# Both gates' input projections moved to the start of a hybrid decoder layer, cut into quarters of the contraction, and the gated merge put on GpSimd

## What is computed

```python
mod = silu(c) @ w_ada + b_ada                  # six vectors of 2048: shift, scale, gain for two sub-layers
h = rmsnorm(x, g_pre_mix) * (1 + sc_m) + sh_m
hq, hf, hi, hg, cq, ckv, kr, gate_a, gate_b = split(h @ w_in)
y_a = hgrn2(hq, hf, hi, hg) @ w_o_hg           # gated linear recurrence, 16 heads
y_b = attention(cq, ckv, kr) @ w_o_mla         # latent attention, 16 heads
merged = sigmoid(gate_a) * y_a + sigmoid(gate_b) * y_b
x = x + ga_m * rmsnorm(merged @ w_out, g_post_mix)
h = rmsnorm(x, g_pre_ffn) * (1 + sc_f) + sh_f
x = x + ga_f * rmsnorm((silu(h @ w_gate) * (h @ w_up)) @ w_down, g_post_ffn)
```

## Time and profile before

| | us |
|---|---|
| median of three runs | 2020.46 |
| span of the profiled execution | 2021.7 |
| TensorE busy in it | 1871.2 (93%) |
| VectorE busy | 1342.2 (66%) |
| ScalarE busy | 877.7 (43%) |
| GpSimd busy | 115.0 (6%) |
| moved by DMA | 421.8 MB, 209 GB/s in the mean |

### The profile page before, as it was taken

One profiled execution on the slowest core, in us unless ns is written; L12 is line 12 of the kernel. 1 busy time (PEld: TensorE's weight loads), 2 busy tenths in 40 slices (PEclk: granted clock), 3 DMA queues, 4 the chain that ended last, 5 costly groups with the idle time before them and its releaser, 6 DMA issues.

```text
span 2021.7 us, 26141 instructions
## 1 busy us (share of the span) xinstructions
PE 1871.2 (93%) x8954; PEld 1562.8 (77%) x8954; DVE 1342.2 (66%) x1484; ACT 877.7 (43%) x974; POOL 115.0 (6%) x77
## 2 busy tenths in 40 slices
PE   1539999999999999999999996999999999999996
PEld 1428888788878887888787785788888888888885
DVE  7876777687777776777777645655555555555554
ACT  4125364446445643554434443444444443444342
POOL 0000031004000400040000000000000000000000
PEclk8769999999999999999999998999999999999998
DMA  8885754784477448645777654455565555555552
GB/s 320 305 293 192 277 177 148 243 292 161 156 273 269 146 161 287 230 156 167 270 266 276 216 192 172 151 193 188 188 194 189 192 189 191 192 190 187 196 188 73
DMA packets 116225, 421.77 MB, mean 209 GB/s; under 512 B 12976, under 2 KB 13104, under 8 KB 115888
## 3 DMA queue, kind: packets, MB, share of 16 engines
q1 hardware_dynamic: 116144, 420.70, 61.5%
HBM read 418.55 MB, written 2.10 MB: 208 GB/s over the span
## 4 chain that ended last, share of the span: by engine, by line
PE 78%; DVE 9%; DMA 8%; issue 3%; ACT 1%; DVEq 0%; SPq 0%; POOL 0%; ACTq 0%; POOLq 0%
PE PS L677 23%; PE PS L679 23%; PE PS L678 23%; DMA ada_raw<-in_ada 5%; DVE ada_acc L1077 3%; PE PS L862 2%; DMA raw<-in_ada 2%; DVE ada_acc L987 2%; PE PS L686 1%; DVE wlo L973 1%; PE PS L807 1%; PE PS L806 1%; DMA raw<-in_w_c 1%; PE PS L712 1%; ACT whi L377 0%
## 5 line engine op out<-in xcount | busy, mean ns | idle before, releaser
L973 DVE TENSOR_TENSOR wlo<-raw,whi 128x1024 fp32r<-128x1024 f32 (+1 forms) x600 | 734.2, 1228 | 436.6 <-ACT whi L377 427.8
L377 ACT ACTIVATE whi<-raw 128x1024 fp32r<-128x1024 f32 (+1 forms) x600 | 629.7, 1053 | 821.9 <-PE PS L679 675.3
L677 PE MATMUL PS<-whi,hT_hi 128*128 128x512 f32 x1664 | 662.6, 398 | 55.4 <-DVE hT_lo L1057 40.6
L679 PE MATMUL PS<-whi,hT_lo 128*128 128x512 f32 x1664 | 653.0, 392 | 0.0
L678 PE MATMUL PS<-wlo,hT_hi 128*128 128x512 f32 x1664 | 652.8, 392 | 0.0
L677 PEld LDWEIGHTS PS<-whi,hT_hi 128*128 128x128 f32 x1664 | 316.0, 190 | 123.5 <-DVE hT_lo L1057 40.9
L679 PEld LDWEIGHTS PS<-whi,hT_lo 128*128 128x128 f32 x1664 | 315.4, 190 | 67.1
L678 PEld LDWEIGHTS PS<-wlo,hT_hi 128*128 128x128 f32 x1664 | 316.3, 190 | 63.4
L987 DVE SCALAR_TENSOR_TENSOR ada_acc<-ada_raw,csilu,ada_acc 128x512 f32<-128x512 f32 x240 | 180.1, 750 | 55.1 <-DMA ada_raw<-in_ada 50.1
L677 PE MATMUL PS<-whi,oT_hi 128*128 128x512 f32 x480 | 187.6, 391 | 2.4 <-DVE oT_lo L1433 2.4
L679 PE MATMUL PS<-whi,oT_lo 128*128 128x512 f32 x480 | 187.2, 390 | 0.0
(11 more groups left out here) (194 smaller groups left out, 1438.4 us busy)
## 6 DMA issues: line engine op xcount, KB each, us to landing
ada_raw<-in_ada SPq DMA_DIRECT2D x128, 512.0 KB, 4.7
raw<-in_w_gate SPq DMA_DIRECT2D x88, 512.0 KB, 3.3
raw<-in_w_up SPq DMA_DIRECT2D x88, 512.0 KB, 3.3
raw<-in_w_down SPq DMA_DIRECT2D x88, 512.0 KB, 3.3
raw<-in_ada SPq DMA_DIRECT2D x64, 512.0 KB, 4.8
raw<-in_w_hf SPq DMA_DIRECT2D x32, 512.0 KB, 5.5
raw<-in_w_hq SPq DMA_DIRECT2D x32, 512.0 KB, 4.8
raw<-in_w_hi SPq DMA_DIRECT2D x32, 512.0 KB, 4.4
```

The source lines that it names most:

```text
L377: nc.scalar.activation(whi[:, pl.slot(c), 0:w], raw[:, pl.slot(c), 0:w], ACT.Copy)\
L677: nc.tensor.matmul(o, hi[:, kt, tok], whi[:, s, cols], start=start, stop=False)
L679: last = nc.tensor.matmul(o, lo[:, kt, tok], whi[:, s, cols], start=False, stop=stop)
L973: nc.vector.tensor_tensor(wlo[:, s, 0:w], raw[:, s, 0:w], whi[:, s, 0:w].bitcast(F32), ALU.subtract)\
```

## The change

The gates' projections leave the stage of their own and join the latent projections at the start. `w_start` holds, for each quarter of the channels (four k-tiles, two chunks), ten column groups: 2 for cq and ckv, 4 for gate b, 4 for gate a. So the start multiplies 80 chunks in place of 16, in four phases of 20; each phase adds partial sums of two chunks to buffers in SBUF (ScalarE copies in the first phase, VectorE adds in the other three), and sigmoid is taken in place in the last. The gates lie where `ya` and `yb` lay (`gate`), and a new buffer `merged` takes the sum: in the loop VectorE multiplies each output projection by its gate into `scaled`, and GpSimd adds that to `merged`.

A chunk of `w_ada` is now one k-tile of 128 rows by 1024 columns (still 512 KB, one instruction of VectorE in place of two). At the start it goes through four slots of its own, 16 chunks before the first phase and 16 beside the first 16 weight chunks of each of the phases 0 to 2. In the loop 32 chunks go beside c = 3 to 18 and c = 24 to 39 (`ADA_AT`) in place of 24 beside c = 3 to 26. Transposes and gain spreading move between the chunks of the output projection. The masks become bytes, and `pTx` shares memory with `qT`.

```diff
-ADA_A = 3
+ADA_A = 2
+ADA_W = 2 * NW
+ADA_SLOTS = 4
+PH = 4
+SG = 2 + 2 * GD
+W_G = CD // PH
...
+        ADA_AT = [3, 3 * CD]
...
+            def load_ada0(a):
+                if a >= ADA_SLOTS:
+                    sp.wait_ge(ada_step, a - ADA_SLOTS + 1)
+                sp.dma_start(ada0_slot[a % ADA_SLOTS], ada0[a]).then_inc(ada_loaded[a % ADA_SLOTS], 16)
...
             def load(pl, c, src, width=NW):
 
-                sp.wait_ge(lo_ready, pl.through(c) - RING)
+                if not pl.starts(c):
+                    sp.wait_ge(lo_ready, pl.through(c) - RING)
...
+            start = place_c()
+            for c in range(RING):
+                load(start, c, w_start[c])
+            for n in range(PH):
+                for i in range(SG * W_G):
+                    a = (n + 1) * KD + i
+                    if i < KD and a < ADA0:
+                        load_ada0(a)
+                    c = n * SG * W_G + i + RING
+                    if c < N_C:
+                        load(start, c, w_start[c])
...
+                    for d in range(ADA_A):
+                        a = c - ADA_AT[d] - LEAD
+                        if 0 <= a < KD:
+                            load_ada(g, d * KD + a)
...
+                def merge(n):
+
+                    p = pl.pair(8 + n)
+                    pool.wait_ge(pair_free[p], pl.freed(8 + n) + 1)
+                    cols = merged[:, :, n % GD * NW:(n % GD + 1) * NW]
+                    pool.wait_ge(sig("merges"), g * (2 * GD) + (n + 1))
+                    nc.gpsimd.tensor_tensor(cols, cols, scaled[n % 2], ALU.add).then_inc(sig("merges"), 1)
...
+            sum_quarter(0)
+            for n in range(PH):
                 pe.wait_ge(sig("h_low"), (n + 1) * KP_Q)
-                for j in range(2):
-                    multiply(pl, j, CD, 2 * n + 2 * j, 2 * n, 2 * n + 2, hT_hi, hT_lo)
+                for j in range(SG):
+                    multiply(pl, n * SG + j, W_G, (n * SG + j) * W_G, 0, W_G, hT_hi, hT_lo, kt0=n * W_G * KC)
+                    if j == 7 and n < PH - 1:
+                        sum_quarter(n + 1)
...
+            for c in range(CD):
+                pe.wait_ge(sig("m_low"), c + 1)
+                multiply(pl, 0, CD, 0, c, c + 1, hT_hi, hT_lo)
+                if c + 4 < CD:
+                    transpose_merged(c + 4)
+            for j in range(1, GD):
+                if j <= 2:
+                    spread_gain(j)
+                multiply(pl, j, CD, j * CD, 0, CD, hT_hi, hT_lo)
...
+            for a in range(KD):
+                ada0_chunk(a)
+                if a == 3 * KD // 4:
+
+                    dve.wait_ge(sig("x_squared"), TT)
+                    nc.vector.tensor_scalar(stat[:, 0:TT], stat[:, 0:TT], 1.0 / D, EPS, ALU.mult, ALU.add)\
+                      .then_inc(sig("trunk_mean"), 1)
+            shift_and_scale(0)
+            tables()
+            quarter_low(0)
...
+            for c in range(N_C + AHEAD):
+                low(pl, c)
+                n, i = divmod(c, SG * W_G)
+                if i < KD and (n + 1) * KD + i < ADA0:
+                    ada0_chunk((n + 1) * KD + i)
+                if i == SG * W_G - 1 and n < PH - 1:
+                    shift_and_scale(n + 1)
+                    quarter_low(n + 1)
+                j, odd = divmod(c - AHEAD, W_G)
+                if odd == W_G - 1 and SG <= j:
+                    add_pair(pl, j, c - AHEAD, start_sum[j % SG])
...
-                        i = c - A_ADA
-                        if 0 <= i < ADA_A * CD:
-                            j = i // CD
-                            if i == 2 * CD:
-
-                                dve.wait_ge(sig("ada_summed_a"), g + 1)
-                            ada_chunk(g * ADA_A + j, i % CD, j % 2)
+                        for d in range(ADA_A):
+                            a = c - ADA_AT[d]
+                            if 0 <= a < KD:
+                                if d and a == 0:
+
+                                    dve.wait_ge(sig("ada_summed_b"), g + 1)
+                                ada_chunk(g, d * KD + a)
...
-                        add_pair(pl, 8 + n, c - 3, sums_of[:, :, (n % GD) * NW:(n % GD + 1) * NW])
+                        dve.wait_ge(sig("gate_ready"), 2 * GD)
+                        dve.wait_ge(multiplied, pl.through(c - 3))
+                        if n == 1:
+                            dve.wait_ge(sig("cross_scored"), g + 1)
+                        if n >= 2:
+                            dve.wait_ge(sig("merges"), g * (2 * GD) + n)
+                        p = pl.pair(8 + n)
+                        nc.vector.tensor_tensor(scaled[n % 2], banks(2 * p), start_sum[2 + n], ALU.mult)\
+                          .then_inc(pair_free[p], 1)
```

More of the change, by code:

```diff
@@ L416, in _, with scale_quarter @@
             pl = place_c()
-            for n in range(QUARTERS):
-                for c in range(n * W_Q, (n + 1) * W_Q):
-                    high(pl, c)
+            def scale_quarter(n):
                 act.wait_ge(sig("scale_h_ready"), n + 1)
@@ new lines, in kr_multiply @@
+            def kr_multiply():
+                pe.wait_ge(sig("kr_loaded"), 16)
+                for tt in range(TT):
+                    for k in range(KD):
+                        o = PS[:, XB + tt, 0:ROPE]
+                        at = (k % 2) * T + tt * P
+                        last = nc.tensor.matmul(o, xT[:, k // 2, at:at + P], key_weights[:, k * ROPE:(k + 1) * ROPE],
+                                                start=k == 0, stop=k == KD - 1)
+                last.then_inc(sig("kr_multiplied"), 1)
@@ L1557 @@
     ukv = w_ukv.reshape(LORA, heads, 2 * P)
-    ada = _by_columns(w_ada)
     at = 4 * D
```

515 lines of the change are left out of this document (230 added, 285 removed).

## The result

The changed kernel took 2059.8 us (median of 2057.0, 2059.8 and 2066.1) where the kernel before took 2021.7 in the same session: the ratio is 1.020, with a 95% interval of 1.017 to 1.023. The changed kernel is slower by some 38 us. The forecast was 2039 us, 18 us slower than before, with a range from 1998 to 2060: the sign held, but the loss is twice the forecast and stands at the upper end of the range.

A forecast was written before the change was run, and what follows sets the result against it. TensorE, busy 93%, was taken as the bound, so only its idle time could be gained. 2021.7 - 8 (start) + 29 (loop) - 2 (output projection) = 2040.7 us, forecast as 2039 us, 0.9% slower; range 1998 to 2060.

The forecast's parts named there:

- The first product: At the start: TensorE's first product comes at 51 us, against 52.0 before.
- The loads at the start: Start phases: queue order makes VectorE wait for w_ada, L = 5.2 us from low's end to landing; gain 8 us.
- The Trainium skill's landing time: At the start: transfer figure giving L, low's end to w_ada's landing, as 4.55 us; start 15 us shorter than forecast.
- Rival 3: At the start: loads land at 3.8 us, L = 4.55; start ends at 337, total 2025 us; chance 0.15.
- Rival 1: Start runs at VectorE's own pace, loads there when wanted; start ends at 297, total 1986 us; chance 0.13.
- Rivals 2 and 4: 2: added steps hide in the loop, 2012 us, chance 0.12; 4: TensorE's clock falls at start, 2054 us, chance 0.08.
- rival 4: At the start: TensorE's clock falls in half of 24 gaps, some 15 us, total 2054 us; chance 0.08.
- Level 0 and 1: Loop: accumulations ahead of decay(0) make TensorE wait 5.2 us, level 1 1.1, clock and products 0.9; 29 in four passes.
- Nothing elsewhere in a pass: Loop's later levels and freed steps: VectorE's gaps of 1.1 to 2.2 us take the accumulations, so no cost or gain.
- GpSimd's merges: Loop: eight merges a pass at 3.5 us each on GpSimd cost nothing; 14 us if VectorE's cover fails.
- Output projection: Output stage: transposes between chunks take most of TensorE's 3.2 us idle; gain 2 us, moved gain spread even with tail.

The follow-up runs named there:

- e2: Changed kernel with each load of w_ada at the start issued two chunks earlier in SP's queue: 2007.7 us, ratio 0.992.
- e3: Changed kernel with each pass's second accumulation run paused at chunks 28 to 32 and ending at chunk 44 in place of 39: 2040.3 us, ratio 1.008.
- e12: Changed kernel with each GpSimd merge adding only 8 of 512 columns, the rest of the sum left out: 2045.5 us, ratio 1.012.
- e11: Changed kernel with w_ada start loads two chunks earlier, accumulation runs moved (chunks 5-20, 24-27, 33-44), earlier mean, GpSimd merges of 8 of 512 columns: 1951.8 us.

## Why the prediction missed

- **The first product** (forecast 51, before 52.0): 52.3. Right.
- **The loads at the start** (phases of 73.4, 81, 81 and 65 us, gain 8): the phases took 69.6, 76.2, 78.6 and some 67, gain 15.4. The mechanism was right: 24 of the 48 steps wait for more than 1 us (72.37 after 2.67 us, 74.86 without, 80.22 after 2.94; the regular turn of every second step begins in phase 1), 63 us in all, where 24 x (5.2 - 2.61) = 62 was forecast. Mis-sized was VectorE's own work between the waits. The step was set at 2.61 us and the add at 1.25 more; e2 has 2.33 and 1.13. That is 0.56 us for each of 8 pairs and 0.68 for each of 16, 15 us; the three phases took 11 us less than forecast.
- **The Trainium skill's landing time** (L = 4.55, start 337): the measured start lies midway between that and the forecast. (The section gives its figure for transfers that GpSimd issues; SP issues these.) Rival 3, which used this L, had phases of 68.2, 76.2 and 76.2 us, near those measured, but by luck: in phase 2 the time from the end of `low` to the landing was 4.8 us (228.43 to 233.25) and 5.0 (236.80 to 241.78), nearer the forecast's 5.2, and it was the shorter step that brought the phases down. e2 shows that the length of a landing isn't the point: it grew by a third for the weights, and no wait was left.
- **Rival 1** did not come, but its reason was sound: with the order mended the start ends at 288, not at 297. Its phases of 62.8 us at VectorE's pace used the same 6.47 us for a pair; with 5.79 they are 8 x 5.79 + 10.9 = 57.2, and those of e2 took 55.0, 55.5 and 57.1 us. The prediction also left out that VectorE stands up to three chunks ahead: at 2.90 us a chunk against TensorE's 2.72 it loses 2.9 us over 16 chunks, about one chunk, and TensorE did not wait.
- **Rivals 2 and 4**: the added steps did not hide in the loop (4.10 us before level 0), and the granted clock in the phases was 0.94, over the 0.9 that would have spoken for rival 4.
- **Level 0 and 1** (5.2 + 1.1 + 0.9 = 7.2 us a pass): the place and the cause (e3) were right. TensorE's waits for VectorE from c = 28 to level 0 are 0.96 us (at 653.54), 0.21 and 4.10, 5.3 together, where 5.2 was forecast as one. The term for level 1 was mis-sized: it waits for nothing, the clock makes all of its 3.3 us, where 1.1 was set for wait and clock together. The stretches to level 0 and to level 1 are 4.3 + 3.3 = 7.6 us longer, and that leaves out the 1.7 us that e3 gives back ahead of the self scores.
- **Nothing elsewhere in a pass**: this step failed. The second pass is 2.7 us longer ahead of the self scores (1.7 of it these accumulations, as e3 shows), 0.8 at the later levels and 3.6 at its end; there the merges make 2.4 (e12) and the sum of `ada_acc` 0.9 (1.85 us where it took 0.95). It is 1.0 shorter in its first two stretches. Its loss is 13.9 us, the mean of the four passes 11.4; the prediction had 7.2.
- **GpSimd's merges, "I cost it at nothing"**: the step that failed most. It was 13 to 18 us (e12, e11), and the bound of 14 that was kept for it was near. The row that was used (a `low` of 1.68 us beside a difference of 1.77) already had one engine waiting for the other: GpSimd's difference from 664.75 ended at 665.78, and the `low` begun at 665.19 ended 1.09 us behind it. It was read as a small rate loss instead of a turn taken. By turns, a merge of 2.4 us holds a `low` for 2.1, VectorE's group takes 5.60 us against TensorE's 5.44, and the slack that was pleaded (VectorE waits on ScalarE there) is gone; in e12 it is back, 1.22 us ahead of the `low` at 737.13.
- **Output projection** (gain 2): 7.6 us longer, with 1.5 back in the rest. The moved spread of 3.57 us is in it; it was set even against the tail, which gave back only 1.5. TensorE waits 4.2 us for the first merged rows, since `low` and merge take turns right to the end. With the narrowed merge (e12) the wait is 0.33 us and the stage 114.0. Why the tail got back only 1.5 of 3.57 us was not tried.
